# A router and expert stage: first pair's rows picked on TensorE, its weights used by feature halves, five more weight places, plain products queued after the token rows

## The reference, cut to what matters

```python
def expert_choice_ffn(h, w_router, w_gate, w_up, w_down):
    cap = CAPACITY * N // N_EXPERTS
    aff = jax.nn.softmax((h @ w_router).astype(f32), -1)
    gate, idx = lax.top_k(jnp.swapaxes(aff, 1, 2), cap)
    xg = h[bidx, idx]
    g = jnp.einsum('becd,edf->becf', xg, w_gate)
    u = jnp.einsum('becd,edf->becf', xg, w_up)
    y = jnp.einsum('becf,efd->becd', jax.nn.silu(g) * u, w_down) * gate[..., None].astype(h.dtype)
    return jnp.zeros_like(h).at[bidx, idx].add(y)
```

## Time and profile before

| what | us |
|---|---|
| median of 3 runs (lowest, highest) | 2253.85 (2251.12, 2254.5) |
| the profiled execution's own time | 2257.76 |
| its span, first to last instruction | 2256.4 |
| TensorE busy in it | 2149.8 |
| granted TensorE clock, mean | 0.989 |

### The profile page before, as it was taken

The page is one execution under the profiler, slowest core; times in us unless marked ns, Lnnn a source line. Parts: engine busy times, 40 slices in busy tenths (PEclk is TensorE's granted clock), DMA queues, the critical chain, the costliest instruction groups (busy, mean ns, idle before and its releaser), DMA issues.

```text
span 2256.4 us, 31283 instructions
## 1 busy us (share of the span) xinstructions
PE 2149.8 (95%) x12021; PEld 1684.0 (75%) x12021; DVE 1435.3 (64%) x2588; ACT 948.8 (42%) x1641; POOL 593.0 (26%) x366
## 2 busy tenths in 40 slices
PE   7999998789998999999999999999999999999999
PEld 4786787543436776777889999987677677899997
DVE  4844547722326877675687676769666765877674
ACT  4444544411114456445344333444554544434442
POOL 0111134010001554330003444245433200234450
PEclk9999999989999999999999999999999999999999
DMA  8217311599994232221324223232222123333321
GB/s 308 67 47 233 122 38 49 224 362 409 409 409 143 66 94 57 69 73 56 103 85 140 78 93 112 75 100 75 68 64 76 56 75 94 112 112 113 113 75 57
DMA packets 164267, 288.21 MB, mean 128 GB/s; under 512 B 13422, under 2 KB 103064, under 8 KB 164120
## 3 DMA queue, kind: packets, MB, share of 16 engines
q1 hardware_dynamic: 161824, 278.73, 36.5%
q0 software_dynamic: 1152, 4.19, 0.5%
q10 hardware_dynamic: 1144, 3.29, 0.4%
HBM read 281.98 MB, written 4.19 MB: 127 GB/s over the span
## 4 chain that ended last, share of the span: by engine, by line
PE 74%; DVE 14%; ACT 4%; DMA 3%; issue 3%; SPq 1%; POOL 0%; DVEq 0%; ACTq 0%
PE PS L766 19%; PE PS L768 19%; PE PS L767 19%; PE PS L2576 4%; PE PS L2617 2%; PE PS L1567 2%; PE PS L1549 2%; PE PS L2637 1%; PE PS L1559 1%; DMA AR<-in_w_mod_dram 1%; PE PS L3374 1%; DVE AL L948 1%; DVE CO L945 1%; SPq L4166 1%; DMA FM<-in_w_up_dram 1%
## 5 line engine op out<-in xcount | busy, mean ns | idle before, releaser
L754 POOL TENSOR_TENSOR WLO<-RAW,WHI 128x1024 fp32r<-128x1024 f32 (+1 forms) x95 | 230.2, 2426 | 520.9 <-ACT WHI L717 514.8
L766 PE MATMUL PS<-OPH,WHI 128*128 128x512 f32 x616 | 255.8, 415 | 5.4 <-DVE AR L1398 2.8
L717 ACT ACTIVATE WHI<-RAW 128x1024 fp32r<-128x1024 f32 (+1 forms) x196 | 204.8, 1050 | 130.5 <-PE PS L768 122.4
L768 PE MATMUL PS<-OPH,WLO 128*128 128x512 f32 x616 | 243.1, 395 | 0.0
L767 PE MATMUL PS<-OPL,WHI 128*128 128x512 f32 x616 | 242.5, 394 | 0.0
L766 PE MATMUL PS<-WHI,OPH 128*128 128x512 f32 (+2 forms) x568 | 225.5, 397 | 10.5 <-DVE OPL L2276 2.5
L766 PE MATMUL PS<-SIDEH,WHI 128*128 128x256 f32 x768 | 217.6, 283 | 1.8 <-DVE WLO L3782 1.8
L767 PE MATMUL PS<-SIDEL,WHI 128*128 128x256 f32 x768 | 217.3, 283 | 0.0
L768 PE MATMUL PS<-SIDEH,WLO 128*128 128x256 f32 x768 | 217.3, 283 | 0.0
L768 PE MATMUL PS<-WHI,OPL 128*128 128x512 f32 (+2 forms) x568 | 215.6, 380 | 0.0
L767 PE MATMUL PS<-WLO,OPH 128*128 128x512 f32 (+2 forms) x568 | 214.7, 378 | 0.0
(11 more groups left out here) (541 smaller groups left out, 4960.9 us busy)
## 6 DMA issues: line engine op xcount, KB each, us to landing
RAW<-in_w_in_dram SPq DMA_DIRECT2D x102, 512.0 KB, 3.7
RAW<-in_w_ffn_in_dram SPq DMA_DIRECT2D x48, 512.0 KB, 4.4
RAW<-in_w_ffn_out_dram SPq DMA_DIRECT2D x44, 512.0 KB, 4.9
XRAW<-in_w_ffn_in_dram SPq DMA_DIRECT2D x40, 512.0 KB, 6.2
RAW<-in_w_mod_dram SPq DMA_DIRECT2D x36, 512.0 KB, 4.8
ONCE<-in_w_down_dram SPq DMA_DIRECT2D x35, 512.0 KB, 15.8
RX<-in_w_gate_dram SPq DMA_DIRECT2D x29, 512.0 KB, 15.1
RAW<-in_w_out_dram SPq DMA_DIRECT2D x24, 512.0 KB, 3.5
```

The lines of the kernel that those rows point to most:

```text
L717: hi.up(A.e.activation(q.fhi, q.flat, ACT.Copy), ("w", q.i))
L754: lo_p.up(G.e.tensor_tensor(q.flo, q.flat, q.fhi.bitcast(F32), ALU.subtract), ("w", q.i))
L766: T.e.matmul(o, a[0], b[0], start=first, stop=False)
L768: return T.e.matmul(o, a[1], b[0], start=False, stop=last)
```

## The change

The first pair's rows no longer go through DRAM: TensorE multiplies the token rows in SBUF with the one-hot rows (`pe_picked`), once for each half of 512 features, and the first `pe_gate_up` uses gate and up of the first half, then of the second: its steps (j, n), j gate or up, n a quarter of the features, are (0,0) (0,1) (1,0) (1,1) (0,2) (0,3) (1,2) (1,3). ACT scales two of the four column blocks of a half and DVE the other two. `onehot` now makes 128 x 128 at a time. The other pairs are still gathered, through one buffer GX and two XG. OH holds one x at a time; the products of `pe_slots` move into the first two `pe_gate_up`. `pe_twos` stands ahead of the token rows, its copy on DVE behind the mask, and `pe_clock_kept` adds seven plain 128x512 products behind the token rows. Places: 37 at the start, and one more from piece 56.

```diff
+    OLD_MASKS = nc.alloc_sbuf_tensor_at("OLD_MASKS", [128, 1024], F32, offset=cx + 4 * CST["lmask"][0])[:, :]
+    OLD_ROOTS = nc.alloc_sbuf_tensor_at("OLD_ROOTS", [128, 1024], F32, offset=rx)[:, :]
+    XTOK = [mem(f"XTOK{t}", at, 1024)[:, :] for t, at in enumerate((1024, 2048, 8704, 9728))]
...
+    PLACES += [Place(once(j), None, n) for j, n in ((4, 128), (5, 128), (6, 152), (7, 152), (10, 192))]
+    user = {h: max(i for i in J["out"][1] if seq[i].half == h) for h in range(NHL)}
+    PLACES += [Place(in_(FM, 3072 + 1024 * h, 1024), user[h], 184) for h in sorted(user, key=user.get)]
     PLACES += [Place(in_(FM, 6144 + 1024 * j, 1024), "out", 192) for j in range(2)]
     PLACES += [Place(XP[:, x, :], "router", n) for x, n in ((0, 40), (1, 64), (4, 40), (5, 64))]
-    PLACES += [Place(once(j), "router", n) for j, n in ((0, 80), (1, 80), (2, 176), (3, 176))]
-    PLACES += [Place(once(j), "stored", n) for j, n in ((8, 176), (9, 176), (10, 192), (11, 192))]
-    PLACES += [Place(once(j), "slots", n) for j, n in ((4, 128), (5, 128), (6, 152), (7, 152))]
+    PLACES += [Place(once(j), "router", n) for j, n in ((0, 80), (1, 80), (2, 176), (3, 176), (8, 176), (9, 176))]
+    PLACES += [Place(OLD_MASKS, "router", 192), Place(OLD_ROOTS, "roots", 192)]
+    PLACES += [Place(once(11), "slots", 192, since=56)]
...
+        def pe_picked(h):
+            T.wait_ge(*moe_v["oh", 0, 0])
+            for x in range(2):
+                b = B.one()
+                B.clear(b)
+                for j in range(2):
+                    o = 512 * h + 256 * x + j
+                    for t in range(4):
+                        T.wait_ge(*copy_a["token rows", t, h])
+                        mm = T.e.matmul(ps(b)[:, 128 * j:128 * j + 128], XTOK[t][:, o:o - j + 256:2],
+                                        OH[:, t, 0:128].bitcast(F32), start=(t == 0), stop=(t == 3))
+                PB["xg", 0, h, x] = b
+                turned.up(mm, ("xg", 0, h, x), *([("xg", 0, h)] if x else []))
...
+        def pe_clock_kept():
+            b = B.one()
+            B.clear(b)
+            for m in range(7):
+                mm = T.e.matmul(ps(b), ident, XT[:, m, :], start=True, stop=True)
...
         def act_gathered(g):
             A.wait_ge(*moe_v["twos"])
+            if g == 0:
+                for h in range(2):
+                    A.wait_ge(*turned["xg", 0, h, 1])
+                    for k in (4 * h + 2, 4 * h + 3):
+                        ins = A.e.activation(XG[:, 0, k, :], ps(PB["xg", 0, h, 1])[:, 128 * (k % 2):128 * (k % 2) + 128], ACT.Identity,
+                                             bias=TWOS[:, 1, k:k + 1], scale=TWOS[:, 0, k:k + 1])
...
         def pool_gathered(g):
             G.wait_ge(*moe_v["index", g // 2])
-            if g >= 3:
-                G.wait_ge(*turned["xg", g - 3, 1])
+            G.wait_ge(*turned["xg", g - 1, 1])
...
         def pe_gate_up(g, amid=lambda x: None):
+            for step, (j, n) in enumerate(gate_up_steps(g)):
+                if g == 0 and (j, n) == (0, 2):
+                    pe_picked(1)
+                if j == 0 and n in (0, 2):
+                    T.wait_ge(*copied["xg", g, n // 2])
+                    if g == 0:
+                        T.wait_ge(*copy_a["xg", 0, n // 2, "rest"])
...
         def pe_moe():
             turned.up(mm, "aff")
             B.give(b, (moe_v, "aff16"))
+            pe_twos()
             pe_token_rows()
-            pe_twos()
+            pe_clock_kept()
             T.wait_ge(*moe_v["mask"])
...
-            for x in range(4):
-                pe_slots(x)
-            pe_gathered(0)
+            pe_picked(0)
+            slots_at = {(0, 4): 0, (0, 7): 1, (1, 0): 2, (1, 4): 3}
             for s in range(9):
                 if s < 7:
-                    pe_gate_up(s)
+                    pe_gate_up(s, lambda x: pe_slots(slots_at[s, x]) if (s, x) in slots_at else None)
                     pe_gathered(s + 1)
...
         def dve_moe():
             step(V.e.tensor_scalar(A16[1], A16[0], 0.0, None, ALU.is_lt), "mask")
+            dve_twos()
             V.wait_ge(*turned["mask"])
...
-            for x in range(4):
-                for q in range(4):
-                    onehot(x, q)
-                if x:
-                    dve_slots(x - 1)
-            dve_slots(3)
-            dve_twos()
-            dve_gathered(0)
+            for j in range(2):
+                onehot(0, j)
+            dve_gathered(0)
+            dve_slots(0)
+            for j in range(2):
+                onehot(1, j)
+            dve_slots(1)
+            for j in range(2):
+                onehot(2, j)
             for s in range(9):
                 if s < 7:
                     dve_gathered(s + 1)
+                if s == 0:
+                    dve_slots(2)
+                    for j in range(2):
+                        onehot(3, j)
+                    dve_slots(3)
```

More of the change, by code:

```diff
@@ L260, in take_half @@
         half_last[h] = nhalf[0]
+        user.half = h
         return HALVES[h]
@@ L349, in body, with __init__ @@
     class Place:
-        def __init__(self, at, after, until, slot=None):
-            self.at, self.after, self.until, self.slot, self.last = at, after, until, slot, None
+        def __init__(self, at, after, until, slot=None, since=0):
+            self.at, self.after, self.since, self.until, self.slot, self.last = at, after, since, until, slot, None
     ring = [Place(None, None, 192, (nslot[0] + j) % (NRAW + NRX)) for j in range(NRAW + NRX)]
@@ L368, in expert_piece @@
         made[0] += 1
-        place = min((x for x in PLACES if j < x.until), key=lambda x: x.last)
+        place = min((x for x in PLACES if x.since <= j < x.until), key=lambda x: x.last)
         first, place.last = place.slot is None, j
@@ L374, in expert_piece, with gate_up_steps @@
         return i
+    def gate_up_steps(g):
+        return [(j, n) for ns in (((0, 1), (2, 3)) if g == 0 else ((0, 1, 2, 3),)) for j in range(2) for n in ns]
     both = lambda w, g, k0, per: [expert_piece(w[0, 2 * g + i, k0:k0 + 128 * per, :], per, w.shape[3]) for i in range(2)]
@@ L378, in body @@
         if g < 8:
-            J["gu", g] = [[both(w, g, 256 * n, 2) for n in range(4)] for w in (d["w_gate"], d["w_up"])]
+            part = {(j, n): both((d["w_gate"], d["w_up"])[j], g, 256 * n, 2) for j, n in gate_up_steps(g)}
+            J["gu", g] = [[part[j, n] for n in range(4)] for j in range(2)]
             for pieces in J["gu", g][0] + J["gu", g][1]:
@@ L477, in body @@
     s_cc, s_id, s_tokens = sem("s_cc"), sem("s_id"), sem("s_tokens")
-    s_rows, s_slots = sem("s_rows"), [sem(f"s_slots{i}") for i in range(3)]
+    s_rows, s_slots = sem("s_rows"), sem("s_slots")
     hi, lo_v, lo_p, zero_p = signal("hi"), signal("lo_v"), signal("lo_p"), signal("zero_p")
@@ L2332, in pe_add_cols @@
             pe_cols(key, columns, rhs, 512, operand, lambda m: [(added, (key, m))], after)
-        SQO = in_(AR1, 16776, 1024).rearrange("p (i n) -> p i n", i=2)
+        SQO = in_(AR2, 1280, 1024).rearrange("p (i n) -> p i n", i=2)
         OUT1 = [[i] for i in J["out"][1]]
@@ L2480, in programs @@
         TWOS = in_(FM, 8680, 16).rearrange("p (a k) -> p a k", a=2)
+        def pe_clock_kept():
[3 more added lines that the diff above has]
+                mm = T.e.matmul(ps(b), ident, XT[:, m, :], start=True, stop=True)
+            prod.up(mm, "clock")
+            B.give(b, (prod, "clock"))
         def pe_twos():
@@ L2774, in pool_moe @@
             G.wait_ge(s_rows, 64)
-            for g in range(8):
+            for g in range(1, 8):
                 pool_gathered(g)
@@ L4151, in sync_engine @@
                     Y.wait_ge(*prod["router"])
-                elif q.after == "stored":
-                    Y.wait_ge(s_rows, 64)
+                elif q.after == "roots":
+                    Y.wait_ge(*turned["rows", "x2"])
+                elif isinstance(q.after, int):
+                    Y.wait_ge(*prod["w", q.after])
                 elif q.after == "slots":
```

89 lines of the change are left out of this document (49 added, 40 removed).

## The result

| | median us (lowest, highest), runs |
|---|---|
| before | 2257.89 (2249.49, 2260.61), 9 |
| after | 2264.14 (2260.89, 2267.28), 9 |

The ratio is 1.0037, 95% interval 1.0026 to 1.0049: slower by 8.4 us (5.9 to 11.1), where +2.1 was forecast. The two medians are 6.2 us apart, which lies in that interval; differences of whole times are given by the ratios from here on, as a share of before's time. The profiled execution of after took 2260.89 us, span 2259.6.

What follows compares the result with a forecast made beforehand. It took the expert stage as bound by TensorE's work, with 8.7 us of slack, and by weight transfers. 1.5 - 1.2 + 5.4 + 3.7 + 1.4 = 10.8, minus 8.7, gave +2.1: median 2255.9 us, range 2249 to 2262.

Steps and rivals of the forecast that it cites:

- Do transfers allow that?: Weight transfers of the expert stage: they come about 2 us later at the last waiting point, the same as TensorE.
- the first reuse: Weight transfers: the first reused place waits for TensorE's release at about 472.1 us, against 471.89 before, +0.2.
- two dry pauses: Weight transfers run out after the first eight released pieces and behind the first group: 1.9 and 1.2 us, 3.1 together.
- The order of banks: Router: the last four token-row turns wait for the twos' copy until about 452.5 us, putting plain products behind the mask.
- rival 3: First pair's picked products are dear, at 0.209 us each, each half 2.4 us longer: +6.9 us; chance 0.20.
- A clock that falls again: A sign in the profile after that would show the forecast wrong; TensorE's clock was taken as full from about 461.5 us.
- -1.2 + 5.4 + 3.7 + 1.4: Expert stream: first gate/up at full clock, second picked half with copies, four slots products, wait for pair 1's gather.
- minus the 8.7 us of waits: Expert stage: TensorE's 14 waits for weight transfers, 8.7 us in all, no longer met and so taken off its delay.
- Rival 2: Router: the plain products do run beside top-k, so the experts start 7.7 us earlier: -7 us; chance 0.11.
- late clock: Router: the clock returns 6 us after dense work begins instead of the 4 taken; 0.5 us.
- the likeliest case: The forecast of +2.1 us for the whole kernel, chance 0.53, taken alone: a median of 2252 to 2259 us.

Runs made afterwards that it cites:

- e3: The changed kernel (after) with the place ONCE11 first used from piece 80 instead of piece 56; 2259.04 us, ratio to before 1.0018.
- e1: The changed kernel (after) with DVE's copy of the twos bank moved from behind the mask to ahead of top-k; 2253.91 us, ratio to before 0.9995.
- e4: The changed kernel (after) with the edits of e1 and e3 together; 2251.9 us, ratio to before 0.9981.
- e8: e4 with first slots product ahead of the second picked half, one-hot rows of x = 2 behind first activations, last two slots products one step later; 2247.55 us, ratio 0.9963.
- e9: e4 with the first pair's rows gathered through DRAM like the others, without picked products; 2250.96 us, ratio to before 0.9981.
- e6: The kernel before with only the seven plain products added, behind the token rows and the twos; 2255.7 us, ratio to before 1.0000.

## Why the prediction was wrong

**The step that failed** is the paragraph on the transfers, "Do transfers allow that?": "So the transfers come about 2 us later at the last waiting point, the same as TensorE". It counted the 37 places, the first reuse, the gathers and two dry pauses, and it left the 38th place out. The section on the change and its diff both name it ("one more from piece 56"), its first event is the slots' products, and the same text had put the four `pe_slots` "in the first two groups". Piece 56 comes up at about 499 and the fourth `pe_slots` is done at 504.9. SyncE's queue is in order, so this one piece held all behind it for 5.8 us. I had no term for the place, as if one more could only be stock; it was a wait. e3 changes this place and nothing else: the stage is 5.0 us shorter, 4.1 of it behind the second gate/up, and the time 4.3 by the ratio.

**What held, from the end of the mask.** The order of banks: the last turns start 0.27 us behind the mask (0.2 forecast), take 0.9 (0.9), the plain products 8.6 (8.1), mask turns to slot numbers 2.4 (2.4), one-hot rows 0.95 (0.9). Then the first `pe_picked` took 5.5 (4.45) and the copies 1.0 (0.85). Sum 19.6 against 17.9 forecast, 3.2 later than before instead of 1.5. The picked products' size was right where the clock was full: the second half took 4.04, 0.122 us from start to start against 0.134 taken, so rival 3 did not come. The Trainium skill ("TensorE: Matmul & The Clock Gate", Back-to-back issue gap) has 81 ns for a sustained stream of 128-column products with their weight loads; the runs don't agree with it here, at 122. (An estimate from that figure, 2.6 us a half, would have lowered the forecast's sum by 3.7 and not by 3.4.) What was missed is the clock: I had it full from the middle of the plain products on. It fell at 460.8, behind mask turns and slot-number products that leave TensorE idle between them (busy 0.68, 0.40 and 0.04 in the three windows before), and that is 1.0 us of the 1.7; the plain products are another 0.5. A clock that falls again was among the prediction's signs of being wrong, and it came.

**Inside the stream** the forecast had -1.2 + 5.4 + 3.7 + 1.4 = 9.3 us from the first expert product to the end of the second gate/up. It was 42.7 against 31.3 before, +11.4; in e3 +10.0. The second `pe_picked` with its copies took 5.0 (5.4), a `pe_slots` 0.98 from start to start, 3.9 for four (3.7), the gather's wait 1.2 (1.4). The rest in after is a second stretch of half clock between 490 and 500 (granted 0.83), in which eight expert records took 2.83 instead of 1.94 and four turns 1.12 instead of 0.66 (e3 has neither), and 0.98 us for DVE, which makes the one-hot rows of x = 2 ahead of the activations.

**The slack was also mis-sized**, "minus the 8.7 us of waits". TensorE of e3 is 13.67 us late at the end of the second gate/up and 1.94 at the last sum, so 11.7 were absorbed. A wait costs more than the idle time put down to it. TensorE's timeline of before shows it:

```profile
640.87 1.94 PE L2617 MATMUL PS<-ONCE,FM 128*64 128x512 f32 x8 [0.16 <-DMA ONCE<-in_w_down_dram]
643.43 1.94 PE L2617 MATMUL PS<-RX,FM 128*64 128x512 f32 x8 [0.62 <-DMA RX<-in_w_down_dram]
```

From start to start that is 2.56 us. Eight records in an unbroken stream take 1.73 (467.44 to 470.90 is 3.46 for 16 in after). So the wait cost 0.83 and not 0.62: the 0.2 us by which eight records last longer (1.94) than the next ones wait to start in an unbroken stream (1.73) is lost too. Fourteen such waits make 2.9, and 8.7 + 2.9 = 11.6. This and the 2.9 us by which TensorE was later than forecast (13.7 against 10.8) cancel in e3; that its +1.9 stands so near +2.1 is partly luck. After was 14.54 us late at the end of the second gate/up and 6.96 at the last sum, so that only 7.6 were absorbed, 4.1 less than in e3; that is what SyncE's wait took back, and it gives +7.0.

**The chances.** 0.26 stood on slower, most of it for rival 3 with its dear products and a late clock. It came out slower by another mechanism than any that I listed, and 2264.14 lies above the upper bound of 2262 and above the likeliest case's 2259. Rival 2 was named rightly as the other side: when e1 and e3 let the products run beside top-k, the stage is 4.6 us shorter than before, not 7.1. The start came 5.6 us earlier and not 7.7, mostly since the clock fell for the picked products all the same. Between the stage (+7.0, and +0.7 behind it) and the measured +8.4 (5.9 to 11.1) nothing is left to explain.

**Where a gain was.** At the end of the second gate/up every changed kernel is later than before, e4 by 6.0 us, e8 by 2.6 and e9 by 2.5. So what they win, they win in the waits for weights behind it, 8.7 us before and 0 to 1.2 once SyncE runs free (e3, e4, e8), 2.9 in e9. The weights come in time for two reasons that no run parts. One is the four places more at the start: four pieces of 1.28 us are 5.1 us of transfers done ahead. e9 speaks for them, since SyncE issues into its first reused place 18.8 us behind the mask, hardly earlier than before (19.6), and its stage is 4.8 us shorter. The other is the earlier start, by which that issue comes 12.8 us behind the mask in e4. The kernel before with the places alone wasn't run, nor which of the places counts for how much. The three moves of e8 give the rest, 8.3 us in all.

## What to carry to other kernels

Before a bank, a buffer or a place is handed out at another point, write down for it who reads it last and where that reader now stands in its own queue; here a copy of 0.17 us, with 8.6 us of products queued behind it, set the start by 8.7 us, and one piece in 192 set the stage by 4. A new place in a stream that is issued in order is only stock if it is free when its turn comes; if its first event has been moved too, it stops everything behind it. And judge work that is to hold the clock by whether the next needed products still find it: here they did not, with 3.4 us (after) to 5 us (e4) of thin work between.

## What the runs showed of the hardware

Six microseconds of dense 512-column products did not carry the full clock over top-k's end. It fell 2.4 us after they ended in e4 (450.7 to 453.1), 3.2 us in after (457.6 to 460.8), though 16x16 turns and 64-column products ran in between, and 4.7 us in e6 (447.6 to 452.4). It came back 5.0 us after dense work began in after (449.0 to 454.0), 4.2 us in e4 (455.7 to 459.9), 5.7 us in e6 (467.1 to 472.8) and 2.5 us in before (468.7 to 471.2), so that a forecast needs a range here. It fell again in the middle of the expert stream of after, at 491.5, in the second of two waits of 1.2 and 1.0 us with eight turns between them; in e8, which has no wait for the gather there, it did not. A wait for a weight cost TensorE about 0.2 us beyond the idle time that the profile notes for it. SyncE issued nothing for 5.8 us while one piece waited for its place; once it was free, seven pieces went out within 3.5 us.
